# A pair's softmax inverses made and moved once, and a new order of steps in the two softmax attentions

## The reference, cut to what matters

```python
z = jnp.einsum("bhqd,bshd->bhqs", q_blk, k) * scale      # mla; fox adds c_q - c_k
p = jax.nn.softmax(jnp.where(allowed, z, -jnp.inf), axis=-1)
o = jnp.einsum("bhqs,bshd->bhqd", p.astype(v.dtype), v)
```

## Time and profile before

| what | us |
|---|---|
| median of 3 runs | 1709.67 (1707.98 to 1710.61) |
| the profiled execution | 1708.22 |
| its span | 1706.3 |
| PE busy | 1676.5 |
| DVE busy | 1285.8 |
| ACT busy | 952.9 |

### The profile page before, as it was taken

How to read it: one execution, slowest core, us unless ns; L and a number is a source line. 1 busy time by engine, 2 the same in 40 slices (tenths; PEclk the granted TensorE clock), 3 DMA queues, 4 the chain that set the end, 5 groups by cost and what they waited for, 6 DMA issues and landing times.

```text
span 1706.3 us, 25098 instructions
## 1 busy us (share of the span) xinstructions
PE 1676.5 (98%) x9279; PEld 1441.0 (84%) x9279; DVE 1285.8 (75%) x2054; ACT 952.9 (56%) x1717; POOL 169.7 (10%) x147
## 2 busy tenths in 40 slices
PE   9999999999999998999999999999999999999998
PEld 7888877878788886789899998878887999999977
DVE  6378877776567887688798986785566979898966
ACT  4267875655436765477546364652235866464655
POOL 2011212000300000220000002420003000000041
PEclk9999999999999999999999999999999999999998
DMA  8222124224243333243233443313322432323621
GB/s 274 81 73 75 40 74 101 84 66 148 75 112 85 87 91 93 75 173 124 75 123 99 124 164 120 109 55 109 111 87 93 156 122 100 99 100 99 236 74 50
DMA packets 158163, 180.72 MB, mean 106 GB/s; under 512 B 22121, under 2 KB 130182, under 8 KB 156262
## 3 DMA queue, kind: packets, MB, share of 16 engines
q1 hardware_dynamic: 150790, 159.22, 30.1%
q10 hardware_dynamic: 7264, 20.05, 3.3%
HBM read 161.96 MB, written 12.63 MB: 102 GB/s over the span
## 4 chain that ended last, share of the span: by engine, by line
PE 82%; DVE 10%; ACT 3%; DMA 2%; issue 2%; POOL 1%; ACTq 0%; DVEq 0%; POOLq 0%; SPq 0%
PE bank L1171 24%; PE bank L1172 24%; PE bank L1173 24%; DMA raw_weights<-in_w_mlp_down 2%; DVE split_weights L2704 2%; PE bank L1520 2%; PE bank L1544 1%; PE bank L1439 1%; POOL ssum L3666 1%; DVE act_b L2704 1%; DVE split_weights L2656 1%; PE bank L1428 1%; DVE work L3087 1%; DVE act_a L2706 1%; PE bank L1557 1%
## 5 line engine op out<-in xcount | busy, mean ns | idle before, releaser
L1171 PE MATMUL bank<-act_a,split_weights 128*128 128x512 f32 (+1 forms) x1360 | 526.0, 387 | 7.5 <-DVE act_a L2704 3.7
L1173 PE MATMUL bank<-act_a,split_weights 128*128 128x512 f32 (+1 forms) x1360 | 519.0, 382 | 0.0
L1172 PE MATMUL bank<-act_a,split_weights 128*128 128x512 f32 (+1 forms) x1360 | 518.6, 381 | 0.0
L1171 PEld LDWEIGHTS bank<-act_a,split_weights 128*128 128x128 f32 x1360 | 256.2, 188 | 60.2 <-issue 6.1
L1173 PEld LDWEIGHTS bank<-act_a,split_weights 128*128 128x128 f32 x1360 | 255.9, 188 | 50.5
L1172 PEld LDWEIGHTS bank<-act_a,split_weights 128*128 128x128 f32 x1360 | 256.3, 188 | 45.2 <-issue 0.2
L1171 PE MATMUL bank<-act_b,split_weights 128*128 128x256 f32 (+1 forms) x648 | 207.3, 320 | 1.2 <-DVE split_weights L3398 1.2
L1173 PE MATMUL bank<-act_b,split_weights 128*128 128x256 f32 (+1 forms) x648 | 206.4, 319 | 0.0
L1172 PE MATMUL bank<-act_b,split_weights 128*128 128x256 f32 (+1 forms) x648 | 206.3, 318 | 0.0
L2646 DVE TENSOR_TENSOR split_weights<-raw_weights,split_weights 128x2048 fp32r<-128x2048 f32 x55 | 127.8, 2323 | 75.2 <-ACT split_weights L1882 62.4
L1882 ACT ACTIVATE split_weights<-raw_weights 128x2048 fp32r<-128x2048 f32 x51 | 97.3, 1908 | 118.4 <-PE bank L1173 118.4
(11 more groups left out here) (357 smaller groups left out, 3221.8 us busy)
## 6 DMA issues: line engine op xcount, KB each, us to landing
raw_weights<-in_w_mlp_up SPq DMA_DIRECT2D x32, 1024.0 KB, 5.3
raw_weights<-in_w_mlp_down SPq DMA_DIRECT2D x32, 1024.0 KB, 5.3
raw_weights<-in_w_in SPq DMA_DIRECT2D x18, 1024.0 KB, 5.2
raw_weights<-in_w_conv_in SPq DMA_DIRECT2D x12, 1024.0 KB, 5.2
raw_weights<-in_w_attn_in SPq DMA_DIRECT2D x16, 512.0 KB, 5.2
raw_weights<-in_w_ple_gate SPq DMA_DIRECT2D x8, 1024.0 KB, 5.1
raw_weights<-in_w_out SPq DMA_DIRECT2D x4, 1024.0 KB, 5.4
raw_weights<-in_w_attn_in SPq DMA_DIRECT2D x4, 1024.0 KB, 5.3
```

The lines of the kernel that those rows point to most:

```text
L1171: nc.tensor.matmul(dst, w[0], a[0], start=first, stop=False)
L1172: nc.tensor.matmul(dst, w[0], a[1], start=False, stop=False)
L1173: mm = nc.tensor.matmul(dst, w[1], a[0], start=False, stop=last)
```

## The change

- One inversion per pair (`n1`, 8 columns of sums) in place of one per head; one transfer out (`d1`) and one back (`b1`) per pair in place of two and two.
- The transfer out now writes the inverses to DRAM in the order of tokens, so one value at a time (the source is 128 partitions of 8 values that go to 8 places each); before, each partition wrote 4 neighbours. The transfer back has as its source two rows, each read 64 times, for 128 partitions; before, it was one row read 64 times for 64 partitions.
- The multiplication then reads both operands in one piece, where before it stepped through the rows by four.
- In the strings of ACT and DVE the steps stand in a new order. `b` is now the last step of its own pair. `k` comes much earlier in the next pair. The maximum `m7` comes ahead of `c3`, and in fox ACT's and DVE's `p4` come ahead of `e6` and `m7`. In fox's pairs 6 and 7 output tile 2 is finished a pair earlier, and pair 7 takes its maxima ahead of the output tiles. PE's strings are not changed.

```diff
-        ACT_FOX = "w0 y0 e0 e1 w1 p0 e2 f1 s2 p1 e3 p2 p3 e4 e5 d0 y1 e6 s3 p4 p5 b0 e7 r0 p6 p7 d1 r1"
+        ACT_FOX = "w0 y0 e0 e1 w1 p0 e2 s2 p1 e3 p2 p3 e4 e5 y1 p4 e6 p5 e7 s3 r0 d1 p6 p7 r1 b1"
-        DVE_MLA = "m0 m1 m2 m3 p0 p1 p2 m4 p3 n0 m5 c0 c1 c2 y1 m6 p4 k0 c3 m7 p5 s2 p6 n1 g0 p7 y2 x0 x1 s3 g1"
+        DVE_MLA = "m0 m1 m2 m3 p0 p1 k0 p2 m4 p3 m5 c0 c1 c2 y1 m6 p4 m7 c3 p5 s2 n1 p6 g0 p7 y2 x0 x1 s3 g1"
...
-                    nc.scalar.dma_start(inverse_rows[hh, :].rearrange("(p j) -> p j", p=P), pair_sums(i, hh))\
-                        .then_inc(inverse_out, 16)
+                    nc.scalar.dma_start(inverse_rows.rearrange("h (j p) -> p h j", p=P), row_sums[:, i % 2, :, :],
+                                        allow_slow_non_contiguous=True).then_inc(inverse_out, 16)
...
-                    nc.scalar.dma_start(inverse_half(hh), inverse_rows[hh, :].partition_broadcast(HD)).then_inc(inverse_back, 16)
+                    nc.scalar.dma_start(sq[:, 0, :], inverse_rows[:, None, :].to_broadcast((2, HD, S))).then_inc(inverse_back, 16)
...
-                def inverse(i, hh):
-                    dve.wait_ge(A["exp"], 8 * i + TT * hh + TT)
-                    V.reciprocal(pair_sums(i, hh), pair_sums(i, hh)).then_inc(A["sum_inverse"], 1)
+                def inverse(i):
+                    dve.wait_ge(A["exp"], 8 * i + 8)
+                    both = row_sums[:, i % 2, :, :]
+                    V.reciprocal(both, both).then_inc(A["sum_inverse"], 1)
...
-                    by_tiles = out_.rearrange("p (j q) -> p j q", j=TT)
-                    V.tensor_tensor(by_tiles, by_tiles, sq[:, 0, :].rearrange("p (q j) -> p j q", j=TT), ALU.mult)\
+                    V.tensor_tensor(out_, out_, sq[:, 0, :], ALU.mult)\
```

More of the change, by code:

```diff
@@ L548, in heads_before, with pairs_before @@
             return h + (MLA_HEADS if kind == "fox" else 0)
+        def pairs_before(kind, i):
+            return i + (MLA_HEADS // 2 if kind == "fox" else 0)
         def pair_sums(pair, hh):
@@ L2245, in pair_of_heads @@
                         elif what == "d":
-                            inverse_to_row(pair, s)
+                            inverses_to_rows(pair)
                         elif what == "b":
-                            inverse_to_half(pair, s)
-                        elif what == "f":
-                            if pair:
-                                inverse_to_half(pair - 1, s)
+                            inverses_to_halves(pair)
                         elif what == "e":
@@ L3134, in pair_of_heads @@
                         elif what == "n":
-                            inverse(pair, s)
+                            inverse(pair)
                         elif what == "k":
```

36 lines of the change are left out of this document (17 added, 19 removed).

## The result

The changed kernel takes 1825.66 us, the median of its runs (1823.87 to 1828.47), against 1709.65 us for the kernel before (1707.98 to 1710.61) on the same chip. The ratio is 1.0684, with a 95% interval of 1.067 to 1.0697. The forecast of 1726 us had the direction right and the size wrong by a factor of seven: 116 us were lost, not 17. The profiled execution has a span of 1826.7 us. These are its busy times and the row of PE's granted clock in 40 slices, to be read beside the earlier trace rows.

The account below looks back on a forecast made before the run. PE, busy 98% of the span, was taken as the bound, so only its waits count. The terms -3.1 + 4.4 + 5.0 + 4.2 + 1.0 + 4.5 + 1.0 gave +17.0 us, a forecast of 1726 us, range 1711 to 1736.

Parts of the forecast that it names:

- Mla, the last maximum (-3.1 us): At mla pairs' ends, `m7` starts over 2 us earlier and PE's three gaps go: a gain of 3.1 us.
- Fox, `p4` ahead of `e6` and `m7` (+4.4 us): In fox pairs, ACT's `p4` waits for `v0`, delaying `m7`, `e7` and `t7`: a loss of 4.4 us.
- the rival in which fox wins: Early maxima win everywhere, closing the gaps in fox and the last pair, with a short transfer back: 1700 us, chance 0.05.
- Fox, the start of a pair (+5 us), with 0.5 us for the small pieces: In fox pairs 1 to 5, ACT waits for `d1` to land before the next pair: 5 us lost, between 0 and 9.
- The transfer back (+9.7 us): Two engines carry it in 7.8 us: losses of 4.2 us in mla, 1.0 in fox pairs 1 to 5, 4.5 in pair 6.
- The last pair (+1.0 us): At fox's end, tile 3's wait goes but `p4` and the transfer back delay others: 1.0 us lost, between -1 and +4.
- One inversion and two transfers fewer (nothing): In all pairs, these steps are hidden off PE's path, so removing them is worth nothing by itself.
- pair 6: In fox, `k0` ahead of `m3` makes the next maximum wait for the transfer back: a loss of 4.5 us.
- The worst one: Transfers back take 10 us or small pieces 2 us more each, so `k0` stops every pair: about 1743 us, chance 0.10.
- The faster one: Early maxima win everywhere if `p4` comes free before `e6` wants it, at 543.4 not 544.92: 1700 us, chance 0.05.

Follow-up runs that it names:

- third kernel: The changed kernel with 16-byte pieces out, strided multiplication and two transfers back, its new orders and single inversion kept: 1711.85 us, 1.0019 of the kernel before.

## Why the prediction was wrong, and what of it held

**Mla, the last maximum (-3.1 us): right.** With both transfers mended the mla stage takes 211.5 us instead of 215.1, and no wait at the last transposes is left. In the changed kernel itself the gain is there and buried: the last transposes of the pair wait for nothing, where the earlier trace rows had 0.97 us.

```profile
340.19 0.68 ACT L2196 ACTIVATE tmp<-bank,negmax 128x512 f32<-128x512 f32 x1
...
341.42 0.60 PE L1543 MATMUL bank<-consts,tmp 128*128 128x128 f32 x4
```

**Fox, `p4` ahead of `e6` and `m7` (+4.4 us): right in mechanism, too small.** ACT idles ahead of `p4` until `v0` ends, and `m7`, `e7` and `t7` follow, with a wait of 1.04 us in every pair from 0 on, close to the 1.2 foreseen:

```profile
590.88 0.28 ACT L2226 ACTIVATE act_b<-bank 128x128 fp32r<-128x128 f32 x1 [2.36 <-PE bank L1556]
...
592.00 0.68 DVE L3071 TENSOR_REDUCE negmax<-bank 128x1 f32<-128x512 f32 x1
...
592.72 0.69 ACT L2196 ACTIVATE tmp<-bank,negmax 128x512 f32<-128x512 f32 x1 [0.72 <-DVE negmax L3071]
...
593.54 0.66 PE L1543 MATMUL bank<-consts,tmp 128*128 128x128 f32 x4 [1.04 <-ACT tmp L2196]
```

Undoing it gave 7.8 us. Against before, the fox stage of the third kernel is 6.3 us longer, where 4.4 was foreseen: the prediction lacked a wait of 0.2 to 0.4 us before `v1` in five of the six looped pairs. The rest of the 7.8 is a gain: with `p4` back behind the early maxima the fox stage is 1.8 us shorter than before, since the gaps of 0.49 us in the earlier trace rows (1.9 us in the earlier trace rows) are gone, which the prediction had given only to the rival in which fox wins.

**Fox, the start of a pair (+5 us), with 0.5 us for the small pieces: the step that failed.** ACT's wait for the landing of `d1`, with everything of the next pair queued behind it, was foreseen. Its size hung on the landing, and the prediction took the landing of 128 pieces plus 0.5 us, 2 us at most. The nearest row, 384 pieces of 64 bytes in 2.3 us, is a load into the chip's on-chip memory and not a store to DRAM, and it bounded the number of pieces and not their neighbourhood in memory; pieces that are 64 bytes apart do land in 2.4 us, 1024 of them. The landing was 10.7 us in median, where 16-byte pieces in the same place need 3.8. This term, put at 5.0 us, was worth 89 to 91 us, by undoing the small pieces with and without the other edit. With the short landing the wait at the pair's start is nothing, below the foreseen 1.0 us a pair. The Trainium skill's rule on a last dimension that isn't contiguous ("DMA: Bandwidth & Descriptors", "Rules for kernel authors") spoke against the right transfer. The page's figure of 10.5 ns a packet, measured there on loads, gave an estimate of 0.7 us; what the 4-byte pieces added here is 6.9 us, ten times that.

**The clock multiplies it.** The prediction priced waits by their length. A wait of 5.8 us was followed by about 6 us at a granted clock of 0.50, and over the kernel PE's busy time rose by 37.5 us on top of 83 us of standing still, 45% more. The earlier trace rows had shown the effect (0.57 in a stretch after a wait), and it was used for the last pair alone.

**The transfer back (+9.7 us): the mechanism right, the size half.** Two engines carry it (a DMA share of 0.12 to 0.13): 7.0 to 7.3 us alone on the chip, 7.5 to 7.8 us from issue to multiplication in mla with 16-byte pieces out, and 7.5 to 9.1 us there in the changed kernel, where 7.8 was taken, against 3.0 to 3.3 us for the same 256 KB with 128 rows leading. The rule of the Trainium skill on how many engines a transfer gets ("DMA: Bandwidth & Descriptors", "Why a DMA increments its semaphore by 16 and not by 1"; the prediction named the section "Queues, rings and completion order" for it) gives the same. Undoing it was worth 22.5 us where the small pieces were gone, and 24.9 us where they were not. By stage the 22.5 us are 7.9 in mla, 7.1 in fox, 7.6 behind it, where the prediction had 4.2 and 5.5, and the rest in the last pair. Term by term, in the kernel with 16-byte pieces out: PE's waits ahead of `v0` in mla are 3.4 us (4.2 foreseen), nothing is seen in fox's pairs 1 to 5 (1.0), pair 6 waits 2.5 us (4.5). What it left out are mla's end (2.85 us), where no work covers the transfer, and the wait of 2.7 us in pair 7 for the copies of SP.

**The last pair (+1.0 us): right in its waits, wrong in its end.** In the third kernel the waits of the pair are 0.88, 2.32 and 0.71 us, 3.9 us in all, where the earlier trace rows had 3.7. But the term held the slow transfer back: 30.8 us from the first scores to the last share, after 29.8 before. With that transfer, in the kernel with 16-byte pieces out, it is 38.3 us (669.32 to 707.63), 8.5 us more: the transfer back was issued 24.6 us after the first scores and not 21, and took 11.2 us to its multiplication and not 7.8. With the fast transfers back the pair's part from fox's last exponential on is 1037.0 us against 1036.1.

**One inversion and two transfers fewer (nothing): not quite.** One inversion and one transfer out fewer cost 3.8 us by themselves, half of it because two issues now fall in one busy place of ACT.

**The sum without the step that failed.** The kernel with 16-byte pieces out and one transfer back is close to the one that was priced. It takes 1734.3 us, 25.9 us more than before on its chip, where the prediction had 17.0. By stage it is 4.3 us in mla (1.1 foreseen), 13.4 in fox (14.9) and 8.5 behind it. That fox comes so near is luck: the pair's start and pair 6 were put too high, `p4` and pair 7 too low.

**The rivals.** The worst one (10 us back, or 2 us more for the small pieces, 1743 us) named both culprits, with too small a price on the second: 2 us a transfer, where 6.9 was measured. The faster one put its turning point at the end of `v0`, and that is where the kernel that gained turns: with `e6` and the maxima ahead of `p4` and fast transfers it takes 1704 us.

## What to carry to other kernels

The store of small pieces here was priced by how near to each other they land, not by their number or bytes: writing a few neighbouring elements of a partition as one piece, and paying 0.4 us for a strided multiplication, beat writing them in the order that is convenient to read. Whoever merges transfers should look at the slowest dimension of what results, and at the engine that must wait for the landing: what stands behind that wait sets its price, and in this kernel the lower clock after PE's waits added 45% to the time by which PE stood still longer. When a change bundles orders and transfers, each half should be run alone: here the transfers held 114 of the 116 us, and under them lay an order that, with fox's `p4` put back, gained 4 us.

## What was not expected of the hardware

128 pieces of 4 bytes next to each other in the scratch memory, 512 bytes in all, took 7.2 to 8.9 us to land, as long as 1024 of them (8.5 to 10.2 us), while 1024 pieces 64 bytes apart took 2.3 to 2.5 us. After about 5.6 us of standing nearly idle PE ran for about 6 us at a granted clock of 0.50.
